# Gate logits by feature, two late chunks in one bank, output weights split one per odd block, and identity products ahead of the first head

## The chip, the cores and the metric

The kernel runs on one core of a Trainium2 chip (trn2). The metric is the device time of one execution in microseconds, lower is better. The time given for a kernel is the median of its runs.

## The reference

Two transformer blocks, one after the other, over 256 tokens of width 1024, in float32. What matters here is the second layer of the first block, native sparse attention (NSA), and what stands just ahead of it:

```python
# first block: layer 0 is differential attention, layer 1 is NSA
mod = c_act @ ada_w[layer] + ada_b[layer]          # six chunks of 1024: shift, scale, gate
h_kv = modulate(rms_norm(x, kv_norm), sh_kv, sc_kv)
kv = h_kv @ w_kv                                   # keys and values of three branches, 1536 columns
hid = gelu(blocks_of_32_tokens(kv[0:2]) @ cmp_w1); k_cmp, v_cmp = hid @ cmp_w2

# NSA: 16 heads of 64, 4 key/value groups
proj = h @ w_in                                    # 1024 columns of q, then 48 gate logits
gates = sigmoid(proj[..., 1024:]).reshape(B, T, G, R, 3)
p_c = softmax(q @ k_cmp) * valid                   # compressed branch, 15 blocks
o_s = softmax(q @ k_slc + bias) @ v_slc            # selected branch: all 4 blocks of 64 at T = 256
o_w = softmax(q @ k_win + bias) @ v_win            # window branch: all of 256 tokens
o = gates[..., 0] * (p_c @ v_cmp) + gates[..., 1] * o_s + gates[..., 2] * o_w
mix = o.reshape(B, T, 1024) @ w_out
```

## The kernel before, in words

Every weight is streamed once from memory by SyncE (SP) in a fixed order, the list `weight_plan`, through a ring of ten slots `wring` of 512 KB each. A load waits until the load ten places before it has been read. For precision each weight piece is split in two: ScalarE (ACT) writes its rounded part to `whi` (line 2743), VectorE (DVE) writes the rest to `wlo` (line 1583), and TensorE (PE) takes three products (lines 542 to 544) per pair of tiles. `whi` and `wlo` hold five pieces, so piece p can be split only when piece p-5 has been read by PE. The load slot of a piece is free once DVE has made its `wlo`.

Each engine's order is written out by hand. `keep_ahead(who, p)` makes ACT or DVE split, at that place of its queue, all pieces up to p+4 that it has not split yet. `bank_full(eng, key)` calls it too, with the last piece that PE had read when it took the bank, and then waits for the bank. Results of PE go to four PSUM banks in strict turn: `bank_take` gives the next one and makes PE wait until the bank's use four places earlier has been drained. Two more pairs, `ps_s` and `ps_p`, have fixed jobs.

The places that the change touches, in the order of time:

- **The opening.** The value projection of the first layer (`a_v`, 128x512 products) is followed by eight heads. For head s, PE does the two pieces of its queries and keys (`qk_piece`, 24 products each), and the scores and turns of earlier heads. Between its splits DVE does `chunk_step` (lines 1629 and 1631), a matrix-vector product with a chunk of `ada_w` that POOL loads into two buffers; a chunk's load is issued when the one two before it has been read.
- **The late chunks.** Chunks 6 to 9 of the second `ada` matrix are made on PE: `late_rows(i)` (line 726) gives row sums in a bank, ACT copies them, `late_columns(i)` (line 740) turns them into four columns in a bank of their own, and DVE's `late_drain(i)` adds the bias. Rows 0 and 1 come before the product `w_kv` 0, the columns 0 and 1 after it. DVE then reads the two banks of `w_kv` 0 into `blocks` (line 2204), and frees each with a small memset (line 2209). Columns 2 stand in block 6 of the NSA loop, columns 3 in block 8.
- **`w_kv` 1 and the compressed branch.** 48 products give `k_slc`, 48 more the values, then `cmp_hidden` (line 1174, 64 columns of the array), `w_kv` 2, and the keys and values of the compressed branch.
- **Queries and gates.** `q_pair(i)` is 48 products of 128x256 for four heads. `by_token(("b_in", 2), ...)` gives the 48 gate logits with the tokens as the loaded operand: for each of two halves of the tokens and eight slices of the depth, three products that load 128x128 of `h` and stream 48 columns. ACT takes the exponential from the two banks (line 3053), DVE adds one and takes the reciprocal (lines 2250 and 2252). Then `cmp_scores(0)` (line 1095), and `q_pair(2)`. On ACT, `cmp_exp(0)` (line 3012) stands behind `q_drain(2)`; DVE's `cmp_weigh(0)` (lines 2277 to 2285) needs it, and PE's `cmp_turn(0)` (line 1107) needs `cmp_weigh(0)`.
- **The NSA loop**, 16 blocks b and two more to finish. PE: scores of block b (line 1122), turn of block b-1's first head (line 1134), mix of block b-2 (lines 1154, 1158), half of a side job, turn of block b-1's second head, the other half. Side jobs: blocks 0 to 3 the last queries, 4 to 7 `late_rows` 2 and 3, from 8 on the output product `b_out` with `o_part`. Block 2 has `gate_rows` (line 633), whose bank DVE reads at the end of block 4 (`gate`, line 1908). DVE: scores with bias (line 2301), copy of the turned head (line 2326), splits, and `nsa_weigh` (lines 2310 to 2319). ACT: exponentials (line 3026), copy (line 3034), splits.

Number the pieces so that the first of `b_in_end` is p0: then p0 and p0+1 are the last query pieces, p0+2 to p0+5 the first four of the output weights, p0+6 and p0+7 the next two. Before the change the loop splits like this on DVE (ACT does the same in even blocks):

```python
if b % 2 and (b < 4 or b >= 8):
    keep_ahead("dve", p0 + (b // 2 if b < 4 else b // 2 - 2))
```

Of the kernel before, what the change touches and what calls it, by code (L numbers as in the profile page):

```python
# [33 lines left out]
P = 128  # L34
D = 1024
T = 256
# [151 lines left out]
def build(nc, dram, out):  # L188
# [15 lines left out]
    with ExitStack() as ctx:  # L204
# [97 lines left out]
        cmask = sb("cmask", [P, 2, TT, NCMP])  # L302
        gates = sb("gates", [P, TT, 48])
        c_stat = sb("c_stat", [P, TT, HEADS])

# [145 lines left out]
        def _(pe):  # L451
# [282 lines left out]

            def late_columns(i):

                bank_emptied(pe, ("late_rows", i))
                b = bank_take(pe, ("late_mod", i))
                for j in range(4):
                    last = nc.tensor.matmul(bank[:, b, j:j + 1], row_sums[i][:, j * P:(j + 1) * P], ones[:, 0:1],  # L740
                                            start=True, stop=True)
                last.then_inc(filled[b], 1)
# [228 lines left out]
            def diff_back(u):  # L971
# [10 lines left out]
                last.then_inc(sem("diff_backed"), 1)  # L982

            for s in range(8):
                b = bank_take(pe, ("a_qk", s))
                qk_piece(s, b, 0)
                if slot_head(s - 2) is not None:
                    diff_turns(slot_head(s - 2))
                if slot_head(s - 1) is not None:
                    diff_scores(slot_head(s - 1))  # L990
                qk_piece(s, b, 1)
                if s == 7:
                    gate_rows("a0", 16)
                if slot_head(s - 3) is not None:
                    diff_back(slot_head(s - 3))
                if slot_head(s - 2) is not None:
                    diff_mix(slot_head(s - 2))
                if s in MOD_SLOTS:
                    mod_columns(matvec_order[MOD_SLOTS.index(s)])
# [44 lines left out]
            by_pairs(("w_kv", 0), h_kv, lambda k: pair_split("kv", k))  # L1044
            for t in range(TT):
                late_columns(t)
            by_feature(("w_kv", 1), h_kv, T, name="k_slc")
# [145 lines left out]
            def cmp_keys():  # L1193
# [17 lines left out]
                last.then_inc(filled[b], 1)  # L1211

            cmp_hidden()
            by_feature(("w_kv", 2), h_kv, T, name="k_win")
# [5 lines left out]
            q_pair(1)  # L1220
            by_token(("b_in", 2), h, KT)
            cmp_scores(0)
            q_pair(2)

# [10 lines left out]
            for b in range(18):  # L1235
# [6 lines left out]
                if b == 2:  # L1242
                    gate_rows("n1", 64 + 16)
                if b in (6, 8):
                    late_columns(b // 2 - 1)
                if b == 8:
# [311 lines left out]
        def _(dve):  # L1558
# [7 lines left out]
            def settle():  # L1566
                dve.wait_ge(done, n_done[0])
# [618 lines left out]
            keep_ahead("dve", last + 1)  # L2186
            def late_drain(i):
                key = ("late_mod", i)
                src = bank_full(dve, key)
                at = col["ada_b1"] + 24 + 4 * i  # L2190
                v.tensor_tensor(mod[:, 4 * (22 + i):4 * (23 + i)], src[:, 0:4], params[:, at:at + 4],
                                ALU.add).then_inc(drained[uses[key][0]], 1)
                bank_emptied(dve, key)
                v.memset(stat[:, 1:2], 0.0).then_inc(mod_drained, 1)

# [14 lines left out]
            late_drain(0)  # L2210
            late_drain(1)
            keep_ahead("dve", first_piece[("w_kv", 1)])
# [33 lines left out]
            v.memset(table_raw, 0.0).then_inc(sem("table_clear"), 1)  # L2246
            for t in range(TT):
                bank_full(dve, ("b_in", 2, "tok", t))
                bank_emptied(dve, ("b_in", 2, "tok", t))
            link(v.tensor_scalar(gates[:, :, :], gates[:, :, :], 1.0, None, ALU.add))  # L2250
            settle()
            link(v.reciprocal(gates[:, :, :], gates[:, :, :]))
            gates_v = gates[:, :, :].rearrange("p t (h c) -> p t h c", c=3)
# [79 lines left out]

            cmp_centre(0)
            cmp_weigh(0)
            p0 = first_piece[("b_in_end", 1)]
            for b in range(18):
                if b in (7, 9):
                    late_drain((b - 3) // 2)
                if b < 16:  # L2340
# [3 lines left out]
                if b == 6:  # L2344
                    cmp_centre(1)
                if b % 2 and (b < 4 or b >= 8):
                    keep_ahead("dve", p0 + (b // 2 if b < 4 else b // 2 - 2))
                if b < 16:
# [340 lines left out]
        def _(act):  # L2689
# [360 lines left out]
            q_drain(1)  # L3050
            for t in range(TT):
                src = bank_full(act, ("b_in", 2, "tok", t))
                a.activation(gates[:, t, :], src[:, 0:48], ACT.Exp, scale=-1.0).then_inc(
                    drained[uses[("b_in", 2, "tok", t)][0]], 1)
            q_drain(2)
            cmp_exp(0)
            p0 = first_piece[("b_in_end", 1)]
            for b in range(18):
# [7 lines left out]
                if b >= 3 and b % 2:  # L3066
                    nsa_high((b - 3) // 2)
                if b % 2 == 0 and (b < 4 or b >= 8):
                    keep_ahead("act", p0 + (b // 2 if b < 4 else b // 2 - 2))
                if b == 4:  # L3070
# [449 lines left out]
```

## Time and profile before

| | |
|---|---|
| runs of the kernel before | 1393.14, 1397.04 and 1397.21 us, median 1397.04 |
| profiled execution | 1393.21 us, its span 1391.4 us |
| TensorE | busy 1305.4 us, 94% of the span |
| VectorE | busy 883.9 us, 64% |
| ScalarE | busy 683.1 us, 49% |
| GpSimd | busy 138.9 us, 10% |
| mean granted clock of TensorE | 0.969 |
| read from memory | 264.83 MB, 191 GB/s over the span |

All durations here come from the profiled execution. In rows of the trace the first number is the start, the second the busy time of the row. Start-to-start distances of PE rows are what a product costs; the busy time of one is longer, as they overlap. The number in brackets is the engine's idle time before the row, with the instruction that ended it. A granted clock of 1.00 is TensorE at 2.4 GHz, 0.50 is 1.2 GHz.

### The profile page before, as it was taken

What the parts mean: (1) busy time and instruction counts of PE and PEld (TensorE: products, weight loads), DVE (VectorE), ACT (ScalarE), POOL (GpSimd) and SP (SyncE); (2) the same over time, 40 slices, a digit from 0 to 9 for tenths busy, and PEclk for the clock granted to TensorE, in tenths of its full rate; (3) what the DMA queues carried; (4) which work ended last, traced back from release to release, by engine and by line L of the source; (5) the groups of instructions that cost most, each with busy time, mean ns of one, the idle gap of its engine ahead of it and who ended that gap; (6) DMA issues with size and microseconds to landing.
All of it is one profiled execution on the core that took longest, in us unless ns stands there. A gap on an engine that the chain in (4) does not pass through costs nothing. (4 is left out here: it accounts for less than half of the span.)

```text
span 1391.4 us, 22008 instructions
## 1 busy us (share of the span) xinstructions
PE 1305.4 (94%) x8462; PEld 1130.9 (81%) x8462; DVE 883.9 (64%) x1593; ACT 683.1 (49%) x1196; POOL 138.9 (10%) x166
## 2 busy tenths in 40 slices
PE   6889899999989899989999788999999998999999
PEld 2678698999889756889988766798998776798987
DVE  3579799899575468765545665655555655645453
ACT  2546354344364356535454674554444645555442
POOL 0122111011000000111010120011010110011010
PEclk9989999999999799999999999999999999999999
DMA  9997549999489242385654442196555453366650
GB/s 351 345 278 241 167 152 323 331 347 351 162 242 282 71 131 62 107 301 183 195 184 116 125 152 76 57 315 193 182 175 173 136 182 106 120 199 188 190 167 31
DMA packets 144776, 267.42 MB, mean 192 GB/s; under 512 B 11040, under 2 KB 50208, under 8 KB 144288
## 3 DMA queue, kind: packets, MB, share of 16 engines
q1 hardware_dynamic: 138592, 250.94, 56.0%
q0 software_dynamic: 3456, 12.58, 2.8%
q10 hardware_dynamic: 2624, 2.49, 0.5%
q8 instruction: 68, 1.11, 0.3%
q14 instruction: 36, 0.29, 0.1%
HBM read 264.83 MB, written 1.15 MB: 191 GB/s over the span
## 5 line engine op out<-in xcount | busy, mean ns | idle before, releaser
L1583 DVE TENSOR_TENSOR wlo<-wring,whi 128x1024 fp32r<-128x1024 f32 (+1 forms) x376 | 452.7, 1213 | 319.7 <-ACT whi L2743 318.4
L2743 ACT ACTIVATE whi<-wring 128x1024 fp32r<-128x1024 f32 (+1 forms) x376 | 388.4, 1044 | 387.7 <-PE bank L544 140.7
L542 PE MATMUL bank<-h_hi,whi 128*128 128x256 f32 x1216 | 350.6, 288 | 6.1 <-DVE wlo L1583 3.8
L543 PE MATMUL bank<-h_lo,whi 128*128 128x256 f32 x1216 | 347.2, 286 | 0.0
L544 PE MATMUL bank<-h_hi,wlo 128*128 128x256 f32 x1216 | 347.0, 285 | 0.0
L542 PEld LDWEIGHTS bank<-h_hi,whi 128*128 128x128 f32 x1216 | 236.4, 194 | 11.3 <-issue 6.5
L543 PEld LDWEIGHTS bank<-h_lo,whi 128*128 128x128 f32 x1216 | 236.7, 195 | 0.7
L544 PEld LDWEIGHTS bank<-h_hi,wlo 128*128 128x128 f32 x1216 | 236.5, 194 | 0.0
L3399 POOL TENSOR_TENSOR ex<-ex 128x512 f32<-128x512 f32 x64 | 75.5, 1185 | 704.5 <-ACT g_hi L2874 704.5
L542 PE MATMUL bank<-whi,h_hi 128*128 128x512 f32 (+3 forms) x248 | 99.9, 403 | 10.8 <-DVE wlo L1583 7.2
L542 PE MATMUL ps_s<-whi,g_hi 128*128 128x512 f32 x256 | 102.0, 398 | 4.8 <-DVE g_lo L1852 4.8
L542 PE MATMUL ps_p<-whi,g_hi 128*128 128x512 f32 x256 | 101.1, 395 | 0.0
L543 PE MATMUL ps_p<-wlo,g_hi 128*128 128x512 f32 x256 | 100.6, 393 | 0.0
L543 PE MATMUL ps_s<-wlo,g_hi 128*128 128x512 f32 x256 | 100.5, 393 | 0.0
L544 PE MATMUL ps_p<-whi,g_lo 128*128 128x512 f32 x256 | 100.5, 392 | 0.0
L544 PE MATMUL ps_s<-whi,g_lo 128*128 128x512 f32 x256 | 100.3, 392 | 0.0
L544 PE MATMUL bank<-whi,h_lo 128*128 128x512 f32 (+3 forms) x248 | 95.0, 383 | 0.0
L543 PE MATMUL bank<-wlo,h_hi 128*128 128x512 f32 (+3 forms) x248 | 94.8, 382 | 0.0
L1602 DVE SCALAR_TENSOR_TENSOR acc<-wring,c_col,acc 128x512 f32<-128x512 f32 x98 | 83.5, 852 | 2.2
L542 PEld LDWEIGHTS bank<-whi,h_hi 128*128 128x128 f32 x248 | 49.8, 201 | 22.5 <-DVE wlo L1583 7.3
L542 PEld LDWEIGHTS ps_s<-whi,g_hi 128*128 128x128 f32 x256 | 48.6, 190 | 14.1 <-DVE g_lo L1852 4.9
L544 PEld LDWEIGHTS ps_p<-whi,g_lo 128*128 128x128 f32 x256 | 48.6, 190 | 10.3
(395 smaller groups left out, 1849.8 us busy)
## 6 DMA issues: line engine op xcount, KB each, us to landing
wring<-in_mlp_w SPq DMA_DIRECT2D x128, 512.0 KB, 4.6
wring<-in_ada_w SPq DMA_DIRECT2D x72, 512.0 KB, 7.2
wring<-in_mlp_w_in SPq DMA_DIRECT2D x64, 512.0 KB, 4.1
wring<-in_mlp_w_out SPq DMA_DIRECT2D x64, 512.0 KB, 4.1
wring<-in_a_w_in SPq DMA_DIRECT2D x24, 512.0 KB, 10.0
xn<-in_ada_w POOLq DMA_DIRECT2D x24, 512.0 KB, 4.5
wring<-in_moba_w_qkv SPq DMA_DIRECT2D x24, 512.0 KB, 4.2
wring<-in_kv_ada_w SPq DMA_DIRECT2D x16, 512.0 KB, 8.4
```

The lines of the kernel that those rows point to most:

```text
L542: nc.tensor.matmul(out, lh, rh, start=first, stop=False, skip_group_check=mixed)
L543: nc.tensor.matmul(out, lh, rl, start=False, stop=False, skip_group_check=mixed)
L544: return nc.tensor.matmul(out, ll, rh, start=False, stop=last, skip_group_check=mixed)
L1583: v.tensor_tensor(piece_view(wlo, p), raw_view(p), piece_view(whi, p).bitcast(F32), ALU.subtract).then_inc(lo_ready, 1)
L1602: ins = v.scalar_tensor_tensor(a, w, c_col[:, k:k + 1], a, ALU.mult, ALU.add)
L2743: a.activation(piece_view(whi, p), raw_view(p), ACT.Copy).then_inc(hi_ready, 1)
L3399: g_.tensor_tensor(h, h, h, ALU.mult).then_inc(sem("mlp_sq"), 1)
```

## The change

Four edits. Ten identity products are put in front of the loop over the eight heads. `late_columns` takes two chunks at a time and puts their eight columns into one bank; the second pair moves to block 8. The gate logits are made with the weights as the loaded operand (48 columns of the array) and all 256 tokens streamed, copied to SBUF by ACT, and turned by two transposes; `cmp_exp(0)` goes ahead of `q_drain(2)`, and the gates' arithmetic on DVE goes behind `cmp_centre(0)`. The splits of the NSA loop are spread: `p0 + b // 2 - 2` in every block.

```diff
+        logits = att[0:48, 1280:1536]
 ...
-            def late_columns(i):
-                bank_emptied(pe, ("late_rows", i))
-                b = bank_take(pe, ("late_mod", i))
-                for j in range(4):
-                    last = nc.tensor.matmul(bank[:, b, j:j + 1], row_sums[i][:, j * P:(j + 1) * P], ones[:, 0:1], ...)
+            def late_columns(pair):
+                rows = (2 * pair, 2 * pair + 1)
+                for i in rows:
+                    bank_emptied(pe, ("late_rows", i))
+                b = bank_take(pe, ("late_mod", pair))
+                for i in rows:
+                    for j in range(4):
+                        c = 4 * (i % 2) + j
+                        last = nc.tensor.matmul(bank[:, b, c:c + 1], row_sums[i][:, j * P:(j + 1) * P], ones[:, 0:1], ...)
                 last.then_inc(filled[b], 1)
 ...
+            keep_warm(10, ps_p[:, 1, 0:P])
             for s in range(8):
 ...
-            for t in range(TT):
-                late_columns(t)
+            late_columns(0)
             by_feature(("w_kv", 1), h_kv, T, name="k_slc")
 ...
+            def gate_logits():
+                b, p = bank_take(pe, "gate_logits"), piece_wait()
+                wh, wl = piece_view(whi, p), piece_view(wlo, p)
+                for k in range(KT):
+                    last = product(bank[0:48, b, 0:T], (wh[:, k, :], wl[:, k, :]), (h_hi[:, k, :], h_lo[:, k, :]),
+                                   k == 0, k == KT - 1)
+                piece_of["gate_logits"] = p
+                piece_over(last, "gate_logits")
+            def gate_turn():
+                bank_emptied(pe, "gate_logits")
+                b = bank_take(pe, "gate_turn")
+                for t in range(TT):
+                    last = nc.tensor.transpose(bank[:, b, 48 * t:48 * t + 48], logits[:, t * P:(t + 1) * P],
+                                               ident[0:48, 0:48])
+                last.then_inc(filled[b], 1)
 ...
             q_pair(1)
-            by_token(("b_in", 2), h, KT)
+            gate_logits()
             cmp_scores(0)
-            q_pair(2)
+            for n in range(4):
+                q_part(4, n)
+            gate_turn()
+            for n in range(4):
+                q_part(5, n)
 ...
-                if b in (6, 8):
-                    late_columns(b // 2 - 1)
+                if b == 8:
+                    late_columns(1)
 ...   (DVE)
             v.memset(table_raw, 0.0).then_inc(sem("table_clear"), 1)
-            for t in range(TT):
-                bank_full(dve, ("b_in", 2, "tok", t))
-                bank_emptied(dve, ("b_in", 2, "tok", t))
-            link(v.tensor_scalar(gates[:, :, :], gates[:, :, :], 1.0, None, ALU.add))
-            settle()
-            link(v.reciprocal(gates[:, :, :], gates[:, :, :]))
+            keep_ahead("dve", first_piece[("b_in", 2)])
 ...
             cmp_centre(0)
+            bank_emptied(dve, "gate_turn")
+            link(v.tensor_scalar(gates[:, :, :], gates[:, :, :], 1.0, None, ALU.add))
+            settle()
+            link(v.reciprocal(gates[:, :, :], gates[:, :, :]))
+            settle()
             cmp_weigh(0)
 ...
-                if b in (7, 9):
-                    late_drain((b - 3) // 2)
+                if b == 9:
+                    late_drain(1)
-                if b % 2 and (b < 4 or b >= 8):
-                    keep_ahead("dve", p0 + (b // 2 if b < 4 else b // 2 - 2))
+                if b % 2:
+                    keep_ahead("dve", p0 + b // 2 - 2)
 ...   (ACT)
             q_drain(1)
-            for t in range(TT):
-                src = bank_full(act, ("b_in", 2, "tok", t))
-                a.activation(gates[:, t, :], src[:, 0:48], ACT.Exp, scale=-1.0).then_inc(...)
+            src = bank_full(act, "gate_logits")
+            a.activation(logits, src[0:48, 0:T], ACT.Copy).then_inc(drained[uses["gate_logits"][0]], 1)
+            cmp_exp(0)
+            src = bank_full(act, "gate_turn")
+            a.activation(gates[:, :, :], src[:, 0:96].rearrange("p (t c) -> p t c", t=TT), ACT.Exp, scale=-1.0).then_inc(...)
             q_drain(2)
-            cmp_exp(0)
 ...
-                if b % 2 == 0 and (b < 4 or b >= 8):
-                    keep_ahead("act", p0 + (b // 2 if b < 4 else b // 2 - 2))
+                if b % 2 == 0:
+                    keep_ahead("act", p0 + b // 2 - 2)
```

## Rows read from the trace of the kernel before

**Rows 1.** The page: busy time of each engine.

```profile
PE 1305.4 (94%) x8462; PEld 1130.9 (81%) x8462; DVE 883.9 (64%) x1593; ACT 683.1 (49%) x1196; POOL 138.9 (10%) x166
```

**Rows 2.** Timeline of PE in the opening.

```profile
65.43 0.58 PE L542 MATMUL bank<-h_hi,whi 128*128 128x256 f32 x1 [3.77 <-DVE wlo L1583]
70.72 1.09 PE L458 MATMUL bank<-ones,acc 128*128 128x1 f32 x8
...
86.69 0.90 PE L951 MATMUL ps_p<-ident,ex 128*128 128x128 f32 x3 [5.10 <-DVE stat L1574]
```

**Rows 3.** Timeline of DVE in the opening.

```profile
83.72 1.54 DVE L1631 SCALAR_TENSOR_TENSOR acc<-xn,c_col,acc 128x512 f32<-128x512 f32 x2 [1.38 <-DMA xn<-in_ada_w]
```

**Rows 4.** Timeline of PE: eight identity products elsewhere (two records each).

```profile
569.87 1.95 PE L482 MATMUL ps_p<-ident 128*128 128x128 f32 x16
```

**Rows 5.** Windows: busy per engine, then granted clock, DMA share, GB/s.

```profile
404.00:408.00 4.00, 2.88 (x15) 2.88 (x16) 3.67 (x9) 0.00 (x0) 0.00 (x0) 0.69 1.16 315
420.00:424.00 4.00, 4.00 (x42) 2.63 (x40) 0.00 (x0) 0.03 (x1) 0.00 (x0) 1.00 0.64 208
484.00:488.00 4.00, 4.00 (x21) 3.88 (x23) 3.31 (x17) 1.86 (x8) 0.00 (x0) 0.57 0.71 256
```

**Rows 6.** Timeline of PE around the first late columns.

```profile
400.93 1.84 PE L740 MATMUL bank<-ones,ex 128*128 128x1 f32 x16
405.12 0.38 PE L542 MATMUL bank<-hk_hi,whi 128*128 128x256 f32 x1 [2.35 <-DVE stat L2209]
...
412.46 0.28 PE L542 MATMUL bank<-whi,hk_hi 128*128 128x256 f32 x1
...
418.31 7.13 PE L1174 MATMUL bank<-wring,arena 128*64 128x256 f32 x64
```

**Rows 7.** Timeline of DVE: the second bank of `w_kv` 0 is freed.

```profile
407.88 0.06 DVE L2209 MEMSET stat<- 128x1 f32 x1
```

**Rows 8.** Timeline of PE from the gate logits to the loop.

```profile
450.32 0.19 PE L542 MATMUL bank<-whi,h_hi 128*128 128x48 f32 x1
...
457.81 3.60 PE L1095 MATMUL bank<-k_cmp,arena 64*128 64x15 f32 x32
...
472.49 0.66 PE L1107 MATMUL bank<-ident,extra 128*128 128x128 f32 x4 [2.69 <-DVE extra L2285]
...
505.17 1.96 PE L1095 MATMUL bank<-k_cmp,arena 64*128 64x15 f32 x32
```

**Rows 9.** Timelines of ACT and DVE in the same stretch.

```profile
470.33 0.39 ACT L3012 ACTIVATE extra<-extra 128x240 f32<-128x240 f32 x1
...
458.50 0.75 DVE L2252 RECIPROCAL gates<-gates 128x96 f32<-128x96 f32 x1
...
462.45 0.41 DVE L2269 TENSOR_TENSOR extra<-extra,c_stat 128x240 f32<-128x240 f32 x1
470.76 0.40 DVE L2277 TENSOR_REDUCE c_stat<-extra 128x16 f32<-128x240 f32 x1 [7.91 <-ACT extra L3012]
```

**Rows 10.** Timelines of PE and DVE in blocks 1 and 2.

```profile
483.99 0.89 PE L1134 MATMUL ps_p<-ident,ex 128*128 128x128 f32 x3 [2.09 <-DVE ex L2319]
484.67 3.27 PE L633 MATMUL bank<-ident,mod 128*128 128x128 f32 x16
...
479.58 3.48 DVE L1583 TENSOR_TENSOR wlo<-wring,whi 128x1024 fp32r<-128x1024 f32 x3
```

**Rows 11.** Timelines of PE, ACT and DVE in blocks 4 to 7.

```profile
503.71 0.55 PE L1134 MATMUL ps_p<-ident,ex 128*128 128x128 f32 x3
...
516.55 0.52 PE L1134 MATMUL ps_p<-ident,ex 128*128 128x128 f32 x3 [0.47 <-DVE att L2326]
...
499.72 0.49 ACT L3034 ACTIVATE acc<-ps_p 128x384 f32<-128x384 f32 x1 [0.93 <-PE ps_p L1134]
...
500.16 1.28 DVE L1908 COPY gate_row<-bank 128x512 f32<-128x512 f32 x2
...
502.68 0.55 DVE L2326 COPY att<-ps_p 128x384 f32<-128x384 f32 x1
```

More of the change, by code:

```diff
@@ L733, in late_rows @@
                     last.then_inc(filled[b], 1)
-            def late_columns(i):
-                bank_emptied(pe, ("late_rows", i))
-                b = bank_take(pe, ("late_mod", i))
-                for j in range(4):
-                    last = nc.tensor.matmul(bank[:, b, j:j + 1], row_sums[i][:, j * P:(j + 1) * P], ones[:, 0:1],
-                                            start=True, stop=True)
+            def late_columns(pair):
[6 more added lines that the diff above has]
+                        c = 4 * (i % 2) + j
+                        last = nc.tensor.matmul(bank[:, b, c:c + 1], row_sums[i][:, j * P:(j + 1) * P], ones[:, 0:1],
+                                                start=True, stop=True)
                 last.then_inc(filled[b], 1)
@@ L2186, in _, with late_drain @@
             keep_ahead("dve", last + 1)
-            def late_drain(i):
-                key = ("late_mod", i)
+            def late_drain(pair):
+                key = ("late_mod", pair)
                 src = bank_full(dve, key)
-                at = col["ada_b1"] + 24 + 4 * i
-                v.tensor_tensor(mod[:, 4 * (22 + i):4 * (23 + i)], src[:, 0:4], params[:, at:at + 4],
+                at, to = col["ada_b1"] + 24 + 8 * pair, 4 * (22 + 2 * pair)
+                v.tensor_tensor(mod[:, to:to + 8], src[:, 0:8], params[:, at:at + 8],
                                 ALU.add).then_inc(drained[uses[key][0]], 1)
                 bank_emptied(dve, key)
-                v.memset(stat[:, 1:2], 0.0).then_inc(mod_drained, 1)
+                v.memset(stat[:, 1:2], 0.0).then_inc(mod_drained, 2)
             v.memset(blocks[:, :, :, :, NCMP:16].rearrange("p s l g n -> p (s l) (g n)"), 0.0)
@@ L2210, in _ @@
             late_drain(0)
-            late_drain(1)
             keep_ahead("dve", first_piece[("w_kv", 1)])
@@ L3050, in _ @@
             q_drain(1)
-            for t in range(TT):
-                src = bank_full(act, ("b_in", 2, "tok", t))
-                a.activation(gates[:, t, :], src[:, 0:48], ACT.Exp, scale=-1.0).then_inc(
-                    drained[uses[("b_in", 2, "tok", t)][0]], 1)
+            src = bank_full(act, "gate_logits")
+            a.activation(logits, src[0:48, 0:T], ACT.Copy).then_inc(drained[uses["gate_logits"][0]], 1)
+            cmp_exp(0)
+            src = bank_full(act, "gate_turn")
+            a.activation(gates[:, :, :], src[:, 0:96].rearrange("p (t c) -> p t c", t=TT), ACT.Exp, scale=-1.0).then_inc(
+                drained[uses["gate_turn"][0]], 1)
             q_drain(2)
-            cmp_exp(0)
             p0 = first_piece[("b_in_end", 1)]
```

## The prediction

> **What bounds the kernel now.** I read the page first: PE is busy 94% of the span, so a gain must come from PE's waits, its slow clock, or its own work [rows 1]. Then windows of 4 us, to find where the granted clock is not 1.00. The four edits fall on just such places: 0.69 after the late columns, 0.57 in NSA block 2 [rows 5], and at the gates, where the same scores (line 1095) took 3.60 us that later take 1.96 [rows 8]. Last the timelines of PE, DVE and ACT there, to see who ends each wait. Outside these places PE works without a break through the neighbouring stretches, so what is saved there should shift all that follows. The sum is made against the profiled execution, 1393.2 us. The runs shown lie at 1393.1 and 1397.0 to 1397.2, so the profile is of the faster kind and 3.8 below the median; I carry the difference over to the median.
>
> **Prices of a product.** At the full clock, 48 products of 256 columns took 418.31 - 412.46 = 5.85 us, 0.122 each; at the low one 24 took 70.72 - 65.43 = 5.29, 0.22 each [rows 2, 6].
>
> **Opening: identity products.** Ten are 20 records, by 16 in 1.95 us that is 2.4 us [rows 4]. They stand ahead of head 0's first piece, which now runs without a wait; that piece then ends 2.4 us later, but PE waits 3.77 us behind it for DVE's split of the second, so they are covered [rows 2]. PE then idles 1.4 us instead of 3.8, the clock may stay up, and the second piece takes 24 x 0.122 = 2.9 instead of 5.3; with the eight column records behind it at half their 1.09, up to 2.8 us earlier. What is late next: PE waits 5.10 us at 86.69 for DVE's weights of head 0 [rows 2]. DVE's queue in front of that is set by `chunk_step`, which waits for POOL's loads (1.38 us at 83.72) and not for PE [rows 3]. So the 5.10 grows to about 7.9 and nothing is won. Cost 0; bounds: +2.4 if the cover failed, -2.8 if DVE did follow PE. No wait is added.
>
> **Late columns and `k_slc`.** Counting banks: late rows 0 and 1 take A and B, the two of `w_kv` 0 take C and D. Before, the late columns take A and B, so `k_slc` needs C, which DVE frees only after its first half of `blocks`: PE waits 2.35 us, and the clock falls (0.69 in that window) [rows 5, 6]. After, the eight columns take A, `k_slc` takes B, which ACT emptied before the columns could start, and the values take C and D. PE's 16 column records stay. `k_slc` starts at 400.93 + 1.84 = 402.77, ends 5.85 later at 408.6, after D is free at 407.94 [rows 6, 7]; the values end at 414.5. Before it was 418.31: **3.8 us**, of which 2.35 is the wait and 1.5 the clock (7.34 against 5.85 for `k_slc`). The next work, `cmp_hidden`, has its inputs by 407.9, and the loads of the pieces behind it are released by its own parts, so they move with it. `late_drain(0)` now signals both chunks at once, and no one waits there. Bounds: 0 (if a load sets the end of `cmp_hidden` after all) to 3.8; I take 3.8, since its parts wait for nothing in the rows.
>
> **Gates.** Before, from the first logit product to `cmp_turn(0)`: 472.49 - 450.32 = 22.2 us [rows 8]. In it: 48 logit products in 7.49 us, during which the clock falls; `cmp_scores(0)` at the low clock 3.53 us; `q_pair(2)`, then 2.69 us of waiting. That wait is ACT's `cmp_exp(0)`, done only at 470.33 behind `q_drain(2)`, though DVE had centred the scores at 462.86 [rows 9].
>
> After, in PE's order at the full clock: 24 logit products 2.9; `cmp_scores(0)` 1.8 (1.96 with its overlap, as later at 505.17); `q_part(4)` 2.9; two transposes, at most four records, 0.4; `q_part(5)` 2.9. Sum 10.9, so PE is ready at 461.2. The side chain: scores done 455.1; centre 1.4 (461.41 to 462.86, the same work) to 456.5; exponential 0.4; ACT then splits p0+2, because waiting for the turned bank makes it, 1.05, to 458.0; transposes done 458.2, exponential of 96 columns 0.3; DVE adds (0.2) and takes the reciprocal (0.75) [rows 9], 459.7; `cmp_weigh(0)` 472.49 - 470.76 = 1.73, to 461.4. So `cmp_turn(0)` starts at 461.4 instead of 472.49: **11.1 us**. The added wait is DVE's for the turned gates; behind it stands only `cmp_weigh(0)`, which needs the gates. ACT's copy of the logits (48x256, taken at 0.4 like `cmp_exp`) ends before PE asks for it.
>
> The term's weak point is the clock. With a narrower loaded operand it might not stay up. But `cmp_hidden` loads only 64 columns, runs 7.13 us without a break, and the window inside it has 1.00 [rows 5, 6]. So I take the full clock; the other end is 2.6 us gained: logits 5.3, scores 3.5, queries 10.3, turn 0.5 at 0.22 a product, 19.6.
>
> The same row gives 7.13/64 = 0.111 us for 256 streamed columns on a 64-column load. The Trainium skill (TensorE: Matmul & The Clock Gate, "LDWEIGHTS") says that loading time goes with the loaded operand's columns alone. By that rule the logit products cost 0.111 and not 0.122, and the gain is an estimated 0.3 us more; the row of `cmp_hidden` agrees.
>
> **Splits in the NSA loop.** In block 1 DVE makes three splits in 3.48 us, ahead of its weights; PE waits 2.09 us for those, and the clock falls [rows 10]. With one split, 1.16, the weights come 2.3 us sooner: 2.1 of wait goes. `gate_rows` is 16 records, 3.27 us at the low clock, 1.95 at the full one [rows 4, 10], and turns beside it save 0.2; block 0 a further 0.3. Saved 3.9.
>
> Against it: the pieces don't come one per odd block. DVE reads `gate_rows`' bank at the end of block 4, and `bank_full` there forces the split of p0+4. ACT's half of it is issued only behind its copy in block 4: 499.72 + 0.39, plus 1.05, 501.2 [rows 11]. DVE adds 1.16, then its 1.28 for the bank, to 503.7, where it was 501.44; scores and copy (501.44 to 503.23) 1.8 more, 505.5. PE wanted that copy at 503.71: up to 1.8 us of new wait. In block 6 the next forced split (p0+5, by `cmp_centre(1)`) less a moved `late_drain` (0.3) adds 0.85 to DVE, where PE waited 0.47 already [rows 11]. The two late columns, 0.9 each, now both stand in block 8: taken from a place that DVE bounds, about 0.4 of it is paid. Costs 3.0. Net **0.9**; bounds +3.0 (only costs) to -3.9 (all costs hidden).
>
> **Sum:** 0 + 3.8 + 11.1 + 0.9 = 15.8. Profile 1377.4; median 1397.0 - 15.8 = 1381.
>
> **Rivals.**
> (a) The clock falls in the gates or the first blocks. For it: it fell in this stretch before, with PE just as busy. Fully, the gates give 2.6: 15.8 - 8.5 = 7.3 gained, 1390. For one stretch, like that after the late columns, 1.5 is lost, 1383. The Trainium skill (same page, "A second HAM failure mode: psum-queue depth-cycling") says that small idles between groups of products, cycling through banks, make the clock swing. By that rule blocks 0 and 1 would run low as before. In rows it is the 1.8 of clock in the loop's 3.9, so 1383. Chances 6% full, 16% partial.
> (b) Bank order isn't the wait after the late columns, or a load holds `cmp_hidden`: 3.8 not won, 1385. Against it: DVE's memset ends the wait by name. 9%.
> (c) The identity products do pay, 2.8: 1378. Needs DVE to follow PE in the opening. 6%.
> (d) Slower. In block 1 DVE's splits also free load slots; p0+4's moves from 479.6 to 501.2, some 22 us. SP issues in order, so the next output weights and all MLP weights behind come up to 22 us late. If that MLP starts on an emptied ring, the 22 outweigh the 15.8: 1403. It decides once loads are late by more than 15.8. Against it: measured from the start the loop itself moves 15 us ahead, and ten loads lie ready. 3%.
> (e) The moved splits cost nothing (copies in blocks 4 and 6 are in time): 1378. 8%.
>
> The forecast itself has 52%, its own range 1378 to 1384 (profile kind against median kind included). The time's range, 8 in 10: 1374 to 1390. A change below 0.3% (4.2 us) can't be told from none here. Faster 0.93, same 0.03 (a full clock fall with (b)), slower 0.04.
>
> **What the changed profile would show.** Opening: 20 more records of line 482's kind before head 0, idle before its second piece near 1.4, that piece in 2.9, and a wait of about 8 for DVE behind head 1. `k_slc` starts right behind the 16 column records. One logit group of 24, windows of 1.00 through the gates, no wait over 0.5 before `cmp_turn(0)`, 11 us after the first logit product. PE's 2.09 gone in block 1 and `gate_rows` in 1.95, but new waits of 1 to 2 in block 5 and about 1 in block 7. Wrong would be: 0.50 in the gates' windows, a wait for DVE's memset after the columns, or MLP splits that wait longer for loads than before.

## The result, and the profile after

The changed kernel takes **1379.15 us** (median of 3 runs, 1377.50 to 1379.86) where the kernel before takes 1397.04 (1393.14 to 1397.21): a ratio of 0.9878, 95% interval 0.9849 to 0.9908. The forecast was 1381, range 1374 to 1390. Its profiled execution is the one of 1379.15, span 1377.3; that is 14.06 us below the profiled execution of before (1393.21), and the spans differ by 14.1.

The page of the changed kernel, first section:

```profile
PE 1296.4 (94%) x8460; PEld 1119.8 (81%) x8460; DVE 881.4 (64%) x1589; ACT 684.2 (50%) x1196; POOL 137.1 (10%) x166
```

PE has shed 9.0 us of busy time against [rows 1] with nearly the same number of records (24 logit products fewer; 20 identity records and 2 transposes more): most of it is the same work in more of the full clock.

Timeline of PE in the opening, changed kernel (start, duration, engine, line, operation and tiles; idle before it and who ended it in brackets), the counterpart of [rows 2]:

```profile
59.70 2.39 PE L483 MATMUL ps_p<-ident 128*128 128x128 f32 x20
...
66.75 0.39 PE L543 MATMUL bank<-h_hi,whi 128*128 128x256 f32 x1 [1.79 <-DVE wlo L1611]
...
71.22 0.95 PE L459 MATMUL bank<-ones,acc 128*128 128x1 f32 x8
...
88.44 0.90 PE L956 MATMUL ps_p<-ident,ex 128*128 128x128 f32 x3 [6.50 <-DVE stat L1602]
```

The 20 new records stand ahead of head 0; the idle time after its first piece is 1.79 instead of 3.77. Head 1's turn comes at 88.44 all the same (before 86.69), because DVE's `stat` comes no sooner. DVE there, the counterpart of [rows 3], still waits for POOL's load:

```profile
85.47 1.54 DVE L1659 SCALAR_TENSOR_TENSOR acc<-xn,c_col,acc 128x512 f32<-128x512 f32 x2 [1.48 <-DMA xn<-in_ada_w]
```

Timeline of PE at the late columns, changed kernel (before: [rows 6]). `k_slc` stands right behind the 16 column records without a wait, and from them to `cmp_hidden` it is 13.39 us, where it was 418.31 - 400.93 = 17.38:

```profile
404.72 1.84 PE L745 MATMUL bank<-ones,ex 128*128 128x1 f32 x16
...
406.42 0.36 PE L543 MATMUL bank<-hk_hi,whi 128*128 128x256 f32 x1
...
418.11 7.13 PE L1179 MATMUL bank<-wring,arena 128*64 128x256 f32 x64
```

Timeline of PE from the first of the 24 logit products to `cmp_turn(0)`, changed kernel: 461.31 - 450.12 = 11.19 us, where [rows 8] have 22.17. The scores take 1.96 instead of 3.60, and the turn carries no bracket, so PE did not wait:

```profile
450.12 0.28 PE L543 MATMUL bank<-h_hi,whi 128*48 128x256 f32 x1
...
452.96 1.96 PE L1100 MATMUL bank<-k_cmp,arena 64*128 64x15 f32 x32
...
461.31 0.66 PE L1112 MATMUL bank<-ident,extra 128*128 128x128 f32 x4
```

ACT and DVE beside it, changed kernel (before: [rows 9]). ACT's exponential of the compressed scores runs at 456.41 instead of 470.33; the turned gates reach DVE at 458.55; the last of `cmp_weigh(0)` starts at 460.78, just ahead of PE:

```profile
456.41 0.41 ACT L3039 ACTIVATE extra<-extra 128x240 f32<-128x240 f32 x1 [2.96 <-DVE extra L2291]
...
458.26 0.25 ACT L3082 ACTIVATE gates<-bank 128x96 f32<-128x96 f32 x1 [0.50 <-PE bank L1233]
...
458.55 0.21 DVE L2358 TENSOR_SCALAR gates<-gates 128x96 f32<-128x96 f32 x1 [2.17 <-ACT gates L3082]
458.79 0.75 DVE L2360 RECIPROCAL gates<-gates 128x96 f32<-128x96 f32 x1
...
460.78 0.47 DVE L2307 TENSOR_TENSOR extra<-extra,c_stat 128x120 f32<-128x120 f32 x2
```

Windows of the changed kernel, PE's busy time and records, then granted clock, DMA share and GB/s (before: [rows 5]):

```profile
404.00:408.00 4.00, 4.00 (x37) 1.00 1.10 348
...
452.00:456.00 4.00, 4.00 (x51) 1.00 0.68 218
456.00:460.00 4.00, 4.00 (x34) 1.00 0.05 17
...
484.00:488.00 4.00, 4.00 (x30) 1.00 0.00 0
```

The same windows of the kernel before:

```profile
452.00:456.00 4.00, 4.00 (x27) 0.66 0.61 211
456.00:460.00 4.00, 4.00 (x31) 0.50 0.09 34
```

In the NSA loop the splits gave and took. PE and DVE, changed kernel (before: [rows 10, 11]): `gate_rows` in 1.95 instead of 3.27 and without the wait of 2.09, but two new waits for DVE's copy of `att`, of 1.62 and 1.38, behind splits that a bank forced:

```profile
470.66 1.95 PE L634 MATMUL bank<-ident,mod 128*128 128x128 f32 x16
...
490.06 0.52 PE L1139 MATMUL ps_p<-ident,ex 128*128 128x128 f32 x3 [1.62 <-DVE att L2348]
...
503.02 0.52 PE L1139 MATMUL ps_p<-ident,ex 128*128 128x128 f32 x3 [1.38 <-DVE att L2348]
```

```profile
485.92 1.22 DVE L1611 TENSOR_TENSOR wlo<-wring,whi 128x1024 fp32r<-128x1024 f32 x1 [1.01 <-ACT whi L2770]
487.06 1.28 DVE L1936 COPY gate_row<-bank 128x512 f32<-128x512 f32 x2
...
495.84 1.22 DVE L1611 TENSOR_TENSOR wlo<-wring,whi 128x1024 fp32r<-128x1024 f32 x1
496.97 0.47 DVE L2282 TENSOR_TENSOR extra<-bank,cmask 128x120 f32<-128x120 f32 x2
```

**Where the time went, by stretches.** Executions of one kernel differ by up to 14 us here (25 runs of the kernel before on one chip: 1386.1 to 1400.0), so parts of the change are compared by the lengths of stretches within a trace, between starts of PE's records. A: first late column to `cmp_hidden`. B: first logit product to `cmp_turn(0)`. C: `cmp_turn(0)` to `cmp_turn(1)` (the NSA loop to block 8). D: first late column to the identity products that close the attention part (line 483; before 569.87 [rows 4]).

| kernel | A | B | C | D |
|---|---|---|---|---|
| before | 17.38 | 22.17 | 47.54 | 168.94 |
| changed | 13.39 | 11.19 | 46.09 | 152.53 |
| change | -3.99 | -10.98 | -1.45 | -16.41 |

The stretch from A's end to B's start is 32.01 in both, and behind C 49.84 and 49.85. The first late column itself came at 404.72 instead of 400.93, 3.79 later, and from the closing products to the end it was 820.05 instead of 821.53. -16.41 + 3.79 - 1.48 = -14.10, the difference of the spans.

### The profile page after: what moved, and what is told of

The parts are those of the page before. It is cut to its first block, busy times and chain, and to the rows that moved or that the text cites. A ratio compares the mean times of both kernels' runs of the same rounds, so it can differ in the third digit from the quotient of the medians.

```text
span 1377.3 us, 22000 instructions
## 1 busy us (share of the span) xinstructions
PE 1296.4 (94%) x8460; PEld 1119.8 (81%) x8460; DVE 881.4 (64%) x1589; ACT 684.2 (50%) x1196; POOL 137.1 (10%) x166
## 3 DMA queue, kind: packets, MB, share of 16 engines
q10 hardware_dynamic: 2624, 2.49, 0.6%
## 4 chain that ended last, share of the span: by engine, by line
PE 75%; DVE 10%; ACT 5%; issue 4%; DMA 4%; POOL 1%; SPq 1%; DVEq 0%; ACTq 0%; POOLq 0%
PE bank L543 13%; PE bank L545 13%; PE bank L544 13%; PE ps_s L543 4%; PE ps_s L545 4%; PE ps_s L544 4%; PE ps_p L543 4%; PE ps_p L544 4%; PE ps_p L545 4%; DVE wlo L1611 2%; DMA xn<-in_ada_w 2%; ACT whi L2770 2%; PE ps_s L1320 1%; DVE acc L1659 1%; DMA wring<-in_ada_w 1%
## 5 line engine op out<-in xcount | busy, mean ns | idle before, releaser
L543 PE MATMUL bank<-h_hi,whi 128*128 128x256 f32 (+1 forms) x1224 | 351.0, 287 | 4.1 <-DVE wlo L1611 1.8
L544 PE MATMUL bank<-h_lo,whi 128*128 128x256 f32 (+1 forms) x1224 | 347.7, 284 | 0.0
L545 PE MATMUL bank<-h_hi,wlo 128*128 128x256 f32 (+1 forms) x1224 | 347.6, 284 | 0.0
L543 PEld LDWEIGHTS bank<-h_hi,whi 128*128 128x128 f32 (+1 forms) x1224 | 235.7, 193 | 9.2 <-issue 6.4
L544 PEld LDWEIGHTS bank<-h_lo,whi 128*128 128x128 f32 (+1 forms) x1224 | 235.7, 193 | 0.7
L545 PEld LDWEIGHTS bank<-h_hi,wlo 128*128 128x128 f32 (+1 forms) x1224 | 235.7, 193 | 0.0
L543 PE MATMUL bank<-whi,h_hi 128*128 128x512 f32 (+2 forms) x232 | 95.0, 410 | 10.3 <-DVE wlo L1611 6.9
L544 PE MATMUL bank<-wlo,h_hi 128*128 128x512 f32 (+2 forms) x232 | 90.0, 388 | 0.0
L545 PE MATMUL bank<-whi,h_lo 128*128 128x512 f32 (+2 forms) x232 | 89.9, 388 | 0.0
L543 PEld LDWEIGHTS bank<-whi,h_hi 128*128 128x128 f32 x232 | 45.8, 197 | 21.9 <-DVE wlo L1611 7.0
```

The lines of the kernel that those rows point to most:

```text
L543: nc.tensor.matmul(out, lh, rh, start=first, stop=False, skip_group_check=mixed)
L544: nc.tensor.matmul(out, lh, rl, start=False, stop=False, skip_group_check=mixed)
L545: return nc.tensor.matmul(out, ll, rh, start=False, stop=last, skip_group_check=mixed)
```

## The experiments

"Gained" stands for shorter than in the kernel named. Whole-kernel ratios are to the kernel before on the same chip.

**1. The pair of late columns alone** (label pair_only), the kernel before with this part of the diff:

```
-            for t in range(TT):
-                late_columns(t)
+            late_columns(0)
...
-                if b in (6, 8):
-                    late_columns(b // 2 - 1)
+                if b == 8:
+                    late_columns(1)
```

> The kernel before with only the edit of the late columns (two chunks in one bank, the second pair in block 8). Theory: PE's wait of 2.35 us for the memset that frees the first bank of w_kv 0 goes, and the clock stays at 1.00 through k_slc, 1.5 us; 4.0 us between the 16 column records and cmp_hidden. In block 8 up to 0.4 is paid. 3.5 to 4 us faster than before, about 1393 against a median of 1397. Rival: the gain in place needs the next wait to be free too; if the loads of w_kv 2 or the values' banks take the wait over, 0 to 1.5 us faster.

Ratio 0.9961, 0.9940 to 0.9982 (1389.51 against 1393.42). A is 13.38, to 0.01 the changed kernel's. B, untouched, is 20.63 and not 22.17: the clock fell later in it, as the windows of this kernel show against 0.66 and 0.50 before (its B starts at 451.73, that of before at 450.32):

```profile
452.00:456.00 4.00, 4.00 (x35) 0.91 0.68 205
456.00:460.00 4.00, 4.00 (x27) 0.50 0.38 126
```

C is 48.22, 0.7 longer than before, so D gains 4.84. The shared bank alone makes all of A's gain. The clock is low for 10.2 us in B here, and for 13.6 in the profile of before (windows of 1 us).

**2. The gates alone** (gates_only), the kernel before with:

```
-            by_token(("b_in", 2), h, KT)
+            gate_logits()
             cmp_scores(0)
-            q_pair(2)
+            for n in range(4):
+                q_part(4, n)
+            gate_turn()
+            for n in range(4):
+                q_part(5, n)
```

and ACT's and DVE's side of it.

> The kernel before with only the edit of the gates: logits by feature, turned, the exponential of the compressed scores ahead of the third query drain. Theory: 11 us from the first logit product to cmp_turn(0), 11.0 to 11.3 instead of 22.2; in the loop block 0 has the full clock too (about 1), the wait of 2.09 for three splits in block 1 stays. 11 to 13 us faster than before, 1384 to 1386 at a median of 1397. Rival: the clock that fell in this stretch falls anyway at another place, since the stretch begins at another time than in the changed kernel: 6 to 9 us faster.

Ratio 0.9937, 0.9915 to 0.9960 (1384.90 against 1393.42). B is 11.19; A is 17.15; D gains 11.53 against the profile of before. By the medians the gain is 8.5, less than the 11 to 13 expected and within the rival's 6 to 9. But the rival's reason did not occur: the clock is 1.00 in the windows from 412 to 472. What was too large is the price of the old form. B in that form is 22.17 in the profile of before and 20.58 to 20.63 in the three other traces that have it (pair_only, splits_only, columns_warm); against those the new 11.19 gains 9.4. DVE's three splits in block 1 still cost PE their 2.09:

```profile
473.91 0.55 PE L1135 MATMUL ps_p<-ident,ex 128*128 128x128 f32 x3 [2.09 <-DVE ex L2338]
```

**3. The moved splits alone** (splits_only), the kernel before with:

```
-                if b % 2 and (b < 4 or b >= 8):
-                    keep_ahead("dve", p0 + (b // 2 if b < 4 else b // 2 - 2))
+                if b % 2:
+                    keep_ahead("dve", p0 + b // 2 - 2)
```

and the same for ACT in the even blocks.

> The kernel before with only the splits of the loop spread (p0 + b // 2 - 2 in every block). Theory: block 1 wins the wait of 2.09 us and 1.5 to 2 of clock in block 2; waits for the copies in block 5 (1.6) and block 7 (1.4 instead of 0.47) take 2.5 back, so 1 to 1.5 us faster, hardly to be told from none. Rival: it is a loss, because the moved splits delay ACT and DVE by more than block 1 saves: 1 to 3 us slower. Rival 2: all of 3.9 us is won.

Ratio 0.9985, 0.9962 to 1.0008: no difference that can be told. In place C gains 1.03 (46.51). Timeline of PE: the wait of 2.09 for block 1's weights is gone (that turn is at 485.03, without a bracket), the two turns ahead of it now wait 0.27 and 0.87, and the price stands in blocks 5 and 7, 1.62 and 0.94:

```profile
480.88 0.55 PE L1134 MATMUL ps_p<-ident,ex 128*128 128x128 f32 x3 [0.27 <-DVE ex L2319]
483.01 0.52 PE L1134 MATMUL ps_p<-ident,ex 128*128 128x128 f32 x3 [0.87 <-DVE att L2326]
485.03 0.55 PE L1134 MATMUL ps_p<-ident,ex 128*128 128x128 f32 x3
...
504.82 0.52 PE L1134 MATMUL ps_p<-ident,ex 128*128 128x128 f32 x3 [1.62 <-DVE att L2326]
518.11 0.52 PE L1134 MATMUL ps_p<-ident,ex 128*128 128x128 f32 x3 [0.94 <-DVE att L2326]
```

**4. Wait or clock after the late columns?** (columns_warm), the kernel before with identity products in the second bank ahead of its columns:

```
                 b = bank_take(pe, ("late_mod", i))
+                if i == 1:
+                    keep_warm(10, bank[:, b, P:2 * P])
```

> The kernel before, with ten identity products (20 records) put in front of the second late chunk's columns, writing the bank that the columns then overwrite, so that PE is at work while it would wait for DVE's memset. Theory (of the 3.8 to 4.0 us gained by the shared bank, 2.35 is the wait and 1.5 the clock): the wait shrinks to nearly nothing but the time to k_slc's start stays the same, the clock stays at 1.00, and k_slc takes 5.85 instead of 7.34: columns to cmp_hidden 15.9 instead of 17.38. Rival (the clock falls at this place for another reason than the idle time, as the work before it): k_slc still takes over 7 us and the stretch stays at 17.4.

```profile
402.43 0.95 PE L742 MATMUL bank<-ones,ex 128*128 128x1 f32 x8
403.25 2.48 PE L482 MATMUL bank<-ident 128*128 128x128 f32 x20
405.56 0.95 PE L742 MATMUL bank<-ones,ex 128*128 128x1 f32 x8
406.62 0.39 PE L542 MATMUL bank<-hk_hi,whi 128*128 128x256 f32 x1
...
418.31 0.87 PE L1176 MATMUL bank<-wring,arena 128*64 128x256 f32 x6
```

`k_slc` starts 4.19 us after the first column, as before (405.12 - 400.93), and A is 15.88: 1.50 gained by the clock alone, which is 1.00 in all windows from 400 to 416. The other 2.49 of A's 3.99 is the wait. The 1.50 is that of before's profile: in the two other traces with the old form the wait is again 2.35 and A 17.15 and 18.33, so the clock costs 1.3 to 2.5 there. The whole kernel does not tell (0.9994, 0.9969 to 1.0018).

**5. The logits' form** (logits_by_token), the changed kernel with the logits as before:

```
-            gate_logits()
+            by_token(("b_in", 2), h, KT)
...
-            gate_turn()
```

> The changed kernel with the 48 gate logits computed by token as before (48 products whose streamed operand has 48 columns, twice, one group per token chunk), without the turn, the rest of the new order kept. Theory (the old form itself costs, and pulls the clock down): logits take about 7.5 us instead of 2.8, and behind them the scores 3.5 instead of 1.8 and the first query chunks up to 2.6 more at the low clock; cmp_turn(0) comes 19 to 20 us after the first logit product instead of 11.1. Rival (the clock fell before because of the wait ahead of cmp_turn(0), not because of the logits' form): only the products' own 48 against 24 count, at the full clock about 2.7 us more, cmp_turn(0) at 14, granted clock 1.00 behind.

B is 19.35, 8.16 longer than in the changed kernel: so much hangs on the form of the logits, not on the order behind them. Ratio 0.9955, 0.9927 to 0.9983 (1385.40 against 1392.92). Windows of PE and the scores' row:

```profile
444.00:448.00 4.00, 4.00 (x36) 1.00 1.06 386
448.00:452.00 4.00, 4.00 (x36) 0.92 0.83 285
452.00:456.00 4.00, 4.00 (x21) 0.50 0.47 134
456.00:460.00 4.00, 4.00 (x35) 0.50 0.00 0
```

```profile
456.27 3.60 PE L1100 MATMUL bank<-k_cmp,arena 64*128 64x15 f32 x32
```

PE is busy 4.00 of 4.00 in each window, and the clock falls from 2.4 to 1.2 GHz within the products that stream 48 columns. The scores behind them take the 3.60 of before. The logits last 456.27 - 448.58 = 7.7, against 2.84; the scores lose 1.6, and the remaining 1.7 lies in the query products. While the clock is still full, the old products start 0.112 us apart (448.83 to 451.29, 22 steps), the new ones 0.115 (450.12 to 452.76, 23 steps), though they stream 256 columns and not 48. So an estimated 48 x 0.112 - 2.8 = 2.5 of the 8.2 is the number of products, and the other 5.7 the clock. This edit changes the loaded and the streamed columns and the number of products together; which of them takes the clock down is not shown.

**6. The place of the exponential** (exp_late), the changed kernel with ACT's order as before:

```
-            cmp_exp(0)
             src = bank_full(act, "gate_turn")
...
             q_drain(2)
+            cmp_exp(0)
```

> The changed kernel with ACT's exponential of the compressed scores put back behind the drains of the last two query chunks. Theory (the order of ACT's exponential carries part of the gates' gain): cmp_turn(0) starts 2 to 3 us later after the first logit product than the 11.13 us of the changed kernel, with PE idle just ahead of it, and the clock may fall in the following blocks for another 1 to 2 us. Rival (the gates' gain is all PE's own work and clock, the side chain has room): cmp_turn(0) stays within 0.5 us of 11.1.

```profile
466.72 1.12 PE L1112 MATMUL bank<-ident,extra 128*128 128x128 f32 x4 [2.76 <-DVE extra L2307]
```

B is 13.93, 2.74 longer: the old wait is back (2.69 in [rows 8]), and the clock falls behind it (0.83 and 0.74 in the windows 464 to 472), which makes C 1.18 longer. Ratio 0.9918, 0.9893 to 0.9944. Against the changed kernel, experiments 5 and 6 lose 8.16 and 2.74 in B, together 10.90; it had gained 10.98. That the two agree so closely is in part luck: the clock was low for 13.6 us both in the profile of before and in that of experiment 5, and for 10.2 in the three other traces with the old form.

**7. The identity products** (no_warm, and no_warm_again beside the changed kernel itself, changed_again), the changed kernel without

```
-            keep_warm(10, ps_p[:, 1, 0:P])
```

> The changed kernel without the ten identity products ahead of the first head; the other three edits stay. Changed kernel: 1377.5 to 1379.9 us. Theory: the products are covered by a wait for DVE on either side, so the time is that of the changed kernel, within 1.5 us, 1377 to 1381; head 0's second piece runs at the low clock again (24 products in 5.3 us), and PE's wait for DVE's weights of head 0 shrinks from 6.5 us to about 5. Rival A: the changed kernel stood 3.8 us later than the kernel before when it reached the late columns, because of the products (20 records, 2.4 us, and what they push): then this kernel is 2.5 to 4 us faster, 1374 to 1376. Rival B: the products keep the clock and DVE follows PE: 2 to 3 us slower, 1381 to 1382.

> The changed kernel without the ten identity products ahead of head 0, a second time and beside the changed kernel. Forecast's theory (they are covered by the wait for DVE's second split and win nothing, because DVE's loads set the opening): the median lies within 1 us of the changed kernel's. Rival A (they delay head 0's first piece and with it the opening): 1.5 to 2.4 us faster without them. Rival B (they pay through the clock): 2 to 3 us slower without them.

> The changed kernel unaltered, beside the kernels that differ from it in one part. It is the base of the comparison: 1377 to 1381, with the stretch from the late columns to the closing identity products (152.5 us in its first trace) the same within 0.1 us.

First time: ratio 0.9872, 0.9842 to 0.9901 (1375.53). Second time: 0.9922, 0.9901 to 0.9942 (1380.89), beside the changed kernel's 0.9896, 0.9871 to 0.9921 (1377.90). A, B, C and D are the changed kernel's to 0.06 in all three. Opening of changed_again:

```profile
58.88 2.39 PE L483 MATMUL ps_p<-ident 128*128 128x128 f32 x20
...
65.21 0.39 PE L543 MATMUL bank<-h_hi,whi 128*128 128x256 f32 x1 [1.06 <-DVE wlo L1611]
68.18 0.95 PE L459 MATMUL bank<-ones,acc 128*128 128x1 f32 x8
87.57 0.91 PE L956 MATMUL ps_p<-ident,ex 128*128 128x128 f32 x3 [8.59 <-DVE stat L1602]
```

And of no_warm_again:

```profile
88.53 0.91 PE L956 MATMUL ps_p<-ident,ex 128*128 128x128 f32 x3 [8.43 <-DVE stat L1601]
```

In changed_again the second piece takes 68.18 - 65.21 = 2.97: the clock held, and PE only waits longer. The products do keep the clock there, though not always. Of the six traces with them the piece took 2.97 or 2.98 in four, behind an idle time of 0.81 to 1.67, and about 4.5 in two, behind 1.79 (the first trace of the changed kernel) and 2.10 (exp_late). Of the eight without them it took 4.25 to 5.29 in all, behind 2.81 to 3.77. Nothing comes of it: head 1's turn comes at 86.69 to 88.53 in the eight without the products (mean 87.67) and at 87.35 to 88.74 in the six with them (88.13). The late columns start at 403.2 on average without them and at 404.5 with them, and from the closing products to the end it is 820.6 without and 819.3 with; both differences are smaller than the scatter of single traces with or without them.

The whole kernel leaves a doubt. The first run without them fell to 1375.53, in rival A's range of 1374 to 1376; the second was 3.0 slower than the changed kernel beside it, in rival B's. The pair below has 1.8 slower without them. The two findings are opposite in sign, and no stretch of the traces shows either; it stays open.

**8. The forced splits** (splits_early, and splits_early_again beside the changed kernel), the changed kernel with

```
-                if b % 2:
-                    keep_ahead("dve", p0 + b // 2 - 2)
+                if b % 2 and (b < 4 or b >= 8):
+                    keep_ahead("dve", p0 + (b - 2 if b < 4 else b // 2 - 2), PIECES - (b == 1))
...
+                if b == 2:
+                    keep_ahead("dve", p0)
```

in DVE's loop, and ACT's order of the kernel before (where the expectation has ACT's splits stay, they too went back in this kernel). DVE now makes one split in block 1, two behind the weights of block 2, one in block 3.

> The changed kernel with DVE's output-weight splits moved: p0+2 in block 1, p0+3 and p0+4 behind the weights of block 2, p0+5 in block 3; ACT's stay. Theory (the forced splits make the two new waits): in the changed kernel the split of p0+4 is forced at 485.92 ahead of gate_rows' bank and PE waits 1.62 us at 490.06; the next forced one gives 1.38 at 503.02. With both done earlier, PE's wait in block 5 falls below 0.3 us and the one in block 7 to what the late drain leaves, at most 0.5; the stretch from cmp_turn(0) to cmp_turn(1) gets 2 to 3 us shorter and the whole 2 to 3 faster than the changed kernel. Rival (DVE is the bound of the loop in any case, so its work only changes place): a new wait of the same size appears in blocks 2 to 4, the stretch stays within 0.5 us. Second rival: ACT's own half of p0+4 (issued in block 3 to 4) is the later one, and DVE's move gives under 1 us.

> The changed kernel with the output-weight splits of the NSA blocks done earlier (DVE: one in block 1, two behind the weights of block 2, one in block 3; ACT: in blocks 0 and 2), a second time beside the changed kernel. In its first trace the stretch from the late columns to the closing identity products took 149.8 us instead of 152.5. If nothing behind gives it back, its median is 2.7 us below the changed kernel's; if the loads of the MLP's weights set the rest, it is the same.

```profile
489.28 0.55 PE L1139 MATMUL ps_p<-ident,ex 128*128 128x128 f32 x3
...
501.14 0.52 PE L1139 MATMUL ps_p<-ident,ex 128*128 128x128 f32 x3 [0.27 <-DVE att L2348]
```

```profile
468.93 1.22 DVE L1611 TENSOR_TENSOR wlo<-wring,whi 128x1024 fp32r<-128x1024 f32 x1
...
475.00 2.35 DVE L1611 TENSOR_TENSOR wlo<-wring,whi 128x1024 fp32r<-128x1024 f32 x2
479.32 1.22 DVE L1611 TENSOR_TENSOR wlo<-wring,whi 128x1024 fp32r<-128x1024 f32 x1
```

The 1.62 is gone and of the 1.38 there is 0.27 left; C is 43.29, 2.80 below the changed kernel, and D 149.80 and 149.78. The two splits now lie where DVE idled in the changed kernel, ahead of block 3:

```profile
476.83 0.29 DVE L2323 CUSTOM_DVE_ANT_0 att<-ps_s,bias 128x128 f32<-128x128 f32 x1 [2.65 <-PE ps_s L1127]
```

Ratios 0.9879 (0.9816 to 0.9942) and 0.9882 (0.9861 to 0.9902); beside the changed kernel 1375.27 against 1377.90, 2.6 apart as the stretch says. The intervals overlap, so by the medians alone this is not shown; the stretch shows it.

**9. Both** (splits_early_no_warm): experiment 8 without the identity products.

> Both together: the output-weight splits done earlier, and no identity products ahead of head 0. A version meant to beat both kernels: 2.7 us below the changed kernel by the splits, and a further 0 (the forecast's theory of the opening) to 2.4 us (if the identity products delay it).

Ratio 0.9892, 0.9869 to 0.9914 (1377.10), D 149.75. D is again 2.8 shorter, but the median is only 0.8 below the changed kernel's, where 2.7 or more was expected, and above the 1375.27 of splits_early. What is certain is the loop: with the early splits it is 2.8 shorter than the changed kernel's in all three traces.

## Why the prediction was right, point by point

- **The sum.** 15.8 was forecast for the edits; D, which holds all but the opening, gained 16.41 against the same profile. The profiled execution gained 14.06, since its late columns began 3.79 later than those of before. That is scatter of the stretch ahead: over the fourteen traces they begin between 400.93 and 407.39, and the profile of before is the earliest. Against the medians the gain was 17.9, and in the second comparison on one chip 13.4. The medians of the three single edits were 3.9, 8.5 and 1.4 lower than that of before, 13.8 together. So the mechanism held, but that the total lies so near 15.8 is in part luck: the forecast priced the gates by a trace in which the old form took some 1.6 longer than in three others.
- **Opening, 0.** The step held: head 1's turn waits for DVE, and DVE for loads. The idle time forecast as 1.4 was 1.79, 1.06 in the second trace. The piece in 2.9 and the wait of about 8 came true in the second (2.97, 8.59) but not in the first, where the clock fell nonetheless: 66.75 to 71.22 is 4.47, and the wait 6.50. So the products hold the clock here in four traces of six, not always, at no cost to the sum.
- **Late columns, 3.8.** Measured 3.99 in A. The parts were forecast as 2.35 of wait and 1.5 of clock; experiment 4 gives 2.49 and 1.50. Rival (b), 9%, is out: no wait for a memset or a load is left.
- **Gates, 11.1.** Measured 10.98 against the profile that the forecast was made from, and 9.4 against the old form's other three traces. The new form was priced well: the trace ran by the forecast's times to within 0.5 us: scores done 454.96 (455.1), centred 456.4 (456.5), reciprocal done 459.5 (459.7), turn 461.31 (461.4). That a narrow loaded operand leaves the clock up was argued from `cmp_hidden` alone; it held, with 1.00 in every window. The Trainium skill (TensorE: Matmul & The Clock Gate, "LDWEIGHTS") lets the loading time go with the loaded operand's columns; with the row of `cmp_hidden` that made a logit product 0.111 us. From 450.12 to 452.96 the 24 took 2.84, 0.118 each, between that and the forecast's 0.122. What the forecast didn't separate, experiments 5 and 6 do: taken out of the changed kernel, the logits' form with the clock it costs is worth 8.2, ACT's order 2.7.
- **The loop, 0.9.** Measured 1.45. Saved: from `cmp_turn(0)` to `gate_rows` 12.18 became 9.35, and its 3.27 became 1.95, together 4.15 (3.9 forecast). In it PE waits 0.83 and 0.86 in block 1, where before had only 0.68; the forecast had named no such wait, and more clock won in blocks 0 and 1 made up for it. Costs: a wait of 1.62 in block 5 (1.8), 1.38 - 0.47 = 0.91 in block 7 (0.85), and of the 2.70 in all, 0.17 is left over, which no experiment gives to the late columns (0.4). Experiment 8 shows that the forced splits make the two waits: with them moved, nothing is left of the first, and of the second 0.27, less than the 0.47 of before. Rival (e), that they cost nothing, is out.
- **Rival (a), the clock.** Out for this kernel, full or partial: windows at 1.00 through gates and blocks 1 and 2. The Trainium skill (same page, "A second HAM failure mode: psum-queue depth-cycling") says that small idles between groups of products make the clock swing; by that blocks 0 and 1 would have been slow. They have idles of 0.83 and 0.86 us between groups and stay at 1.00; in experiment 6, behind an idle of 2.76, they are slow.
- **Rival (c).** The place named for it, DVE following PE, is refuted by the opening's rows: where the second piece was 1.3 to 2.3 shorter, head 1's turn came no sooner. That the products pay elsewhere is not (experiment 7).
- **Rival (d), late loads.** Out: behind the closing products it is 820.05 against 821.53, where late loads would have added. Over the fourteen traces this stretch scatters from 816.3 to 823.0. ACT's splits of the MLP weights wait for loads behind the closing products four times on each of the two tensors, 12.3 us in all after the change and 11.1 before, 1.2 more where the rival needed over 15.8.

## What to carry to other kernels

Ask of each slow-clock stretch what form of product stands at its head, not only which wait: here the clock fell within 48 products that stream 48 columns, while PE never idled, and with the operands exchanged (48 columns loaded, 256 streamed) the same sums cost half the products and the clock stayed up. A split or a load that is put off until a bank forces it does not go away: it comes back ahead of the bank's reader, so put it where the engine idles (block 3 here). Where executions scatter by 10 us, compare stretches between fixed records: a sum of steps of 1 us can be verified there and not in the medians. And take the price of a stretch with a falling clock from more than one trace: here one trace of the old form was 1.6 us dearer than three others.

## What the runs showed of the hardware that was not expected

- Stretches at the full clock repeat to 0.06 us or better: A in the new form was 13.38 or 13.39 in ten traces, B in the new form 11.19 or 11.20 in eight. Stretches in which the clock falls don't: A in the old form was 17.38, 17.15 and 18.33, B 22.17, 20.63, 20.61 and 20.58 on unchanged code. So 1.6 of B's 10.98 is that the clock fell early in before's profiled execution and stayed low longer, and the single edits' gains in D (4.84 + 11.53 + 1.62 = 17.99) exceed the 16.41 of all together.
- A product that loads 128 columns and streams 48 costs nearly as much as one that loads 48 and streams 256: 0.112 us from start to start against 0.115, both at the full clock (experiment 5 and the changed kernel).
- Not every wait brings the clock down: in the changed kernel, waits of 1.62 and 1.38 left the clock at 1.00 in every window from 460 to 520, while in before the clock fell behind waits of 2.35, 2.69 and 2.09.
- A clock that falls costs after the wait that goes with it: 2.76 us of idle time cost 2.74 in place and 1.18 behind (experiment 6).
